# A two-block transformer kernel: the second block's first two projections from tokens that are not yet normed

## The chip, the cores and the metric

The kernel runs on one core of a Trainium2 chip. The metric is the device time of one execution in microseconds (us), as the median of several runs. TensorE (PE) multiplies matrices, VectorE (DVE) and ScalarE (ACT) work on elements, GpSimd (POOL) makes the low parts of the weights, and SyncE (SP) issues nearly all loads.

## The reference

256 tokens of 1024 go through a first block (gating, convolution, pooling, feed-forward, a gated embedding) and then through a second one (two kinds of attention, then 32 experts). The change lies at the border: the last step of the first block, and the norm and projection that begin the second.

```
def _rmsnorm(x, g):
    xf = x.astype(jnp.float32)
    y = xf * lax.rsqrt(jnp.mean(xf * xf, axis=-1, keepdims=True) + NORM_EPS)
    return (y * g.astype(jnp.float32)).astype(x.dtype)

def _modulate(h, shift, scale):
    return h * (1 + scale[:, None, :]) + shift[:, None, :]
...
        h = h + jax.nn.sigmoid(h @ w_ple_gate[i]) * (p[i] @ w_ple[i])
...
        h = _modulate(_rmsnorm(x, g_mix[layer]), shift_mix, scale_mix)
        qkv = h @ w_in[layer]
        q_d, k_d, v_d, q_s, k_s, v_s = jnp.split(
            qkv, [D_DIL, 2 * D_DIL, 3 * D_DIL, 3 * D_DIL + D_SB, 3 * D_DIL + 2 * D_SB], axis=-1)
```

`q_s` and `k_s` are the queries and keys of the stick-breaking attention, `q_d` and `k_d` those of the dilated one. For one token the norm is one number r (the inverse root), so a projection of the normed and modulated token is r times the projection of the token times the gain, plus the projection of the shift.

## The kernel before

Every engine has its own instruction list, written out by hand, and waits for the others by semaphores; nothing is scheduled by a planner. The order of the source is the order on each engine.

Products of weights and tokens are done three times, on high and low parts of both operands in the fast format fp32r: high x high, high x low, low x high (`product`, L552 to L554). So every activation matrix needs a high part (ScalarE's copy into the format) and a low part (VectorE's difference), and every weight block likewise (ScalarE's copy L1334, GpSimd's difference L2607). Weights stream through raw buffers and three split buffers; a split waits until the products of three blocks before are done, and ScalarE does two blocks ahead of TensorE (`take`).

The first block ends with `ple_gate`: four pieces of X (`part(n, tt, ...)`: weight part n, token half tt), four PSUM banks `gb`, numbered q = 2 * token half + column half. For each q ScalarE takes the sigmoid in PSUM (`gate`, L1630) and VectorE multiplies by the embedding and adds to X (`gated_embedding`, L2208 and L2210; the semaphore is `x_ok`); the order is q = 0, 2, 1, 3. X holds tokens on the partitions.

The second block begins as follows. TensorE turns the plain tokens (`turn_old`, L874, 16 transposes) for a later residual, which VectorE copies to SBUF as XTO (`old`, L2218). ScalarE sums squares by halves (`half_square`, L1613) and takes roots (`half_root`, L1620), VectorE inverts them. VectorE, and ScalarE for one quarter, multiply the tokens by the inverse root into XN (`normed`, L2235, L1647). TensorE turns XN (`turn_normed`, L887, 16 transposes); ScalarE and VectorE apply gain and shift (columns of MC) from PSUM into HF (L1662, L2248), ScalarE makes the high part (L1667), VectorE the low part (`low_of`, L1899). Then come the projections `qs0`, `ks0`, `qs1`, `ks1`, `qd0`, ... (`qk`, 48 products of 256 columns each, both output halves in one bank); ScalarE copies each result to QK (L1675). `sb_scores(0)` (L936, L937) needs qs0 and ks0; ScalarE's softplus on it is `sb_soft` (L1688 to L1692).

Where ScalarE's list is touched, the split of the ks0 weights has its second half behind the third norm:

```
            gate(1)
            assert begun[0] + 1 == next_split(first["ple_gate"] + 3)
            split_one(third_norm)
```

Behind the attention the experts' weights stream in; their loads wait for the places that the attention leaves.

Of the kernel before, what the change touches and what calls it, by code (L numbers as in the profile page):

```python
# [10 lines left out]
ALU = mybir.AluOpType  # L11
# [211 lines left out]
def program(nc, I, out, const_at):  # L223
    with ExitStack() as ctx:
# [85 lines left out]
        XN = ar(10240, 2048, 2)  # L310
        HF = ar(6144, 2048, 8)
# [81 lines left out]
        def tap(k, c):  # L393
# [24 lines left out]
        so4, so, soe = small(4), small(2), small(2)  # L418

# [14 lines left out]
                 ("norm3", 4), ("heads_s", 2), ("heads_d", 2))  # L434
# [7 lines left out]
         sbs_mm, sv_mm, di_mm, dt_mm, dv_mm, os_mm, xo_mm, cb_mm, ss_mm, rt_mm, hn_mm, rk_mm, ov_mm, xg_mm, gu_mm,  # L442
# [3 lines left out]
            "di_mm dt_mm dv_mm os_mm xo_mm cb_mm ss_mm rt_mm hn_mm rk_mm ov_mm xg_mm gu_mm turn_mm down_mm y0_mm y_mm "  # L446
            ).split())

        (warm_ok, nsq_ok, dg_ok, v_ok, sig_ok, vs_ok, u_ok, z_ok, g_ok, sq_ok, crs_ok, silu_ok, vnorm_ok, ple_ok, post_ok,
         cond_ok, ffa_ok, pg_ok, hfa_ok, qkv_ok, mr_ok, sbe_ok, die_ok, osq_ok, hs_ok,  # L450
         rs_ok, hn_ok, ex_ok, xga_ok, hsa_ok, fin_ok) = (
            sem(n) for n in (
            "warm_ok nsq_ok dg_ok v_ok sig_ok vs_ok u_ok z_ok g_ok sq_ok crs_ok silu_ok vnorm_ok ple_ok post_ok cond_ok "
            "ffa_ok pg_ok hfa_ok qkv_ok mr_ok sbe_ok die_ok osq_ok hs_ok rs_ok hn_ok ex_ok xga_ok "
# [3 lines left out]
        (blank_ok, rv_ok, vst_ok, vn_ok, glu_ok, tap_ok, cs_ok, wst_ok, tab_ok, mix_ok, pools_ok, cc_ok, cn_ok,  # L458
# [4 lines left out]
            "blank_ok rv_ok vst_ok vn_ok glu_ok tap_ok cs_ok wst_ok tab_ok mix_ok pools_ok cc_ok cn_ok bra_ok "  # L463
# [10 lines left out]
        qkv_at = {"qs0": 1, "ks0": 2, "qs1": 3, "ks1": 4, "qd0": 5, "kd0": 6, "qd1": 7, "kd1": 8, "vs": 10, "vd": 12}  # L474
# [42 lines left out]
        def tensor(e):  # L517
# [154 lines left out]
            def wst_sums():  # L672

                w.wait_ge(wst_ok, 1)
                for i in range(2):
# [4 lines left out]
                    free[b] = [(tab_ok, 4 * i + 4)]  # L680
# [178 lines left out]
            part(2, 1, True, True)  # L859
            part(3, 0, True, False)  # L860
            part(3, 1, True, True)
            bb = gb
            for q in range(4):
                free[bb[q]] = [(x_ok, x3(q))]
            held.update(bb)


            def turn_old(tt, half):

                w.wait_ge(x_ok, x3(2 * tt + half))  # L870
# [8 lines left out]
            def turn_normed(bb, tt):  # L879

                w.wait_ge(rv_ok, 8 + 2 * tt)
                for k in range(8):
                    if k == 4 and tt:
                        w.wait_ge(nsq_ok, 15)
# [165 lines left out]
            for kind in ("qs0", "ks0", "qs1"):  # L1050
                qk(kind)
# [1824 lines left out]
```

## Time and profile before

| | us |
|---|---|
| median of 3 runs | 1093.29 (1090.07 to 1094.33) |
| profiled execution, span from the first to the last instruction | 1089.9 |
| TensorE busy | 996.9 (91%) |
| VectorE busy | 528.6 (48%) |
| ScalarE busy | 391.9 (36%) |
| GpSimd busy | 498.4 (46%) |

The page gives the profiled execution by its span; no other time of that execution is listed. Shares of busy time are averages over stages with different limits, and TensorE's are modelled: what counts for a change is which wait ends last at its place. The border of the two blocks lies at 510 to 545 us of the span.

### The profile page before, as it was taken

The page shows a single profiled execution, that of the slowest core. Times are in us where ns is not written, and L with a number is a line of the kernel's source. Part 1 is how long each engine was busy: PE and PEld are TensorE (multiplying, and loading weights), DVE is VectorE, ACT ScalarE, POOL GpSimd, SP SyncE. Part 2 cuts the span into 40 slices and gives each one's busy share as a digit, 9 for nine tenths or more (in the row PEclk, how much of TensorE's full clock was granted, in tenths as well). Part 3 has the DMA queues.
Part 4 walks back from the last instruction along what each step waited for, and adds up shares of the span by engine and source line. Part 5 has one row for each costly group of instructions (what it writes and reads, how often), then busy time and mean ns, then how long its engine had stood idle before and what let it go on. Part 6 is the DMA issues. An engine that isn't in the chain of part 4 may idle for free.

```text
span 1089.9 us, 16602 instructions
## 1 busy us (share of the span) xinstructions
PE 996.9 (91%) x6894; PEld 736.4 (68%) x6894; DVE 528.6 (48%) x980; ACT 391.9 (36%) x559; POOL 498.4 (46%) x210
## 2 busy tenths in 40 slices
PE   7999999999999999999899999999959687859777
PEld 6989988788788888888798895544425243424333
DVE  1998896655367776214358554333213122212114
ACT  7345455554474544446597441000000000000003
POOL 5987699879498887888666510000000000000000
PEclk9999999999999999999999999999989898989889
DMA  9745455546469999638443889999999999999996
GB/s 380 281 166 185 148 201 192 173 190 267 173 232 396 362 362 373 263 116 325 144 155 116 351 347 416 429 425 428 425 429 425 434 427 424 431 426 426 431 422 255
DMA packets 36655, 341.96 MB, mean 314 GB/s; under 512 B 4065, under 2 KB 4449, under 8 KB 6114
## 3 DMA queue, kind: packets, MB, share of 16 engines
q1 hardware_dynamic: 35280, 337.82, 77.6%
q10 hardware_dynamic: 1298, 3.05, 0.7%
q8 instruction: 55, 0.90, 0.3%
q14 instruction: 22, 0.18, 0.0%
HBM read 339.81 MB, written 1.05 MB: 313 GB/s over the span
## 4 chain that ended last, share of the span: by engine, by line
PE 65%; DMA 25%; DVE 6%; ACT 3%; issue 1%; POOL 0%; DVEq 0%; SPq 0%; ACTq 0%
DMA body<-in_gu 21%; PE ps L552 15%; PE ps L554 15%; PE ps L553 15%; PE ps L1201 6%; PE ps L1243 4%; DMA body<-in_dn 4%; PE ps L1232 2%; PE ps L1182 1%; PE ps L734 1%; ACT sph L1334 1%; DVE ar L2314 1%; DVE ar L2308 1%; PE ps L1220 1%; PE ps L787 0%
## 5 line engine op out<-in xcount | busy, mean ns | idle before, releaser
L2607 POOL TENSOR_TENSOR spl<-raw,sph 128x1024 fp32r<-128x1024 f32 x204 | 496.4, 2466 | 139.5 <-ACT sph L1334 139.3
L1334 ACT ACTIVATE sph<-raw 128x1024 fp32r<-128x1024 f32 x204 | 208.3, 1055 | 109.1 <-PE ps L554 91.1
L2615 POOL TENSOR_SCALAR body<-body,SM 128x512 f32<-128x512 f32 x1 | 1.6, 1567 | 447.9 <-DVE SM L1874 447.9
L1826 ACT ACTIVATE ar<-ps 64x256 f32<-64x256 f32 x32 | 12.1, 377 | 332.9 <-PE ps L1201 332.9
L552 PE MATMUL ps<-sph,xbh 128*128 128x512 f32 x304 | 119.6, 394 | 0.4 <-DVE ar L2281 0.4
L554 PE MATMUL ps<-sph,xbl 128*128 128x512 f32 x304 | 118.5, 390 | 0.0
L553 PE MATMUL ps<-spl,xbh 128*128 128x512 f32 x304 | 118.4, 389 | 0.0
L1243 PE MATMUL ps<-ar,ar 128*128 128x512 f32 x240 | 111.6, 608 | 0.0
L552 PE MATMUL ps<-xah,sph 128*128 128x256 f32 x320 | 92.1, 288 | 0.4
L1919 DVE SCALAR_TENSOR_TENSOR ps<-ar,COL,ps 128x256 f32<-128x256 f32 x232 | 92.1, 482 | 0.0
L553 PE MATMUL ps<-xal,sph 128*128 128x256 f32 x320 | 90.5, 283 | 0.0
L554 PE MATMUL ps<-xah,spl 128*128 128x256 f32 x320 | 90.5, 283 | 0.0
L2558 DVE TENSOR_TENSOR ar<-ar,ps 64x256 f32<-64x256 f32 x32 | 13.6, 424 | 141.0 <-ACT ar L1826 141.0
L1243 PEld LDWEIGHTS ps<-ar,ar 128*128 128x128 f32 x240 | 45.4, 200 | 47.5 <-issue 47.5
L552 PE MATMUL ps<-sph,xah 128*128 128x512 f32 x192 | 75.7, 394 | 1.5 <-POOL spl L2607 1.5
L553 PE MATMUL ps<-spl,xah 128*128 128x512 f32 x192 | 74.8, 389 | 0.0
L554 PE MATMUL ps<-sph,xal 128*128 128x512 f32 x192 | 74.8, 389 | 0.0
L1201 PE MATMUL ps<-body,ar 128*32 128x256 f32 x656 | 46.7, 432 | 28.8 <-DMA body<-in_gu 28.8
L2495 DVE COPY ar<-ps 128x128 f32<-128x128 f32 x32 | 9.3, 292 | 127.1 <-PE ps L1220 127.0
L552 PEld LDWEIGHTS ps<-sph,xbh 128*128 128x128 f32 x304 | 57.1, 188 | 12.4 <-DVE ar L2281 0.8
L554 PEld LDWEIGHTS ps<-sph,xbl 128*128 128x128 f32 x304 | 57.1, 188 | 12.1
L553 PEld LDWEIGHTS ps<-spl,xbh 128*128 128x128 f32 x304 | 57.1, 188 | 11.5
(343 smaller groups left out, 1753.6 us busy)
## 6 DMA issues: line engine op xcount, KB each, us to landing
raw<-in_stream SPq DMA_DIRECT2D x127, 1024.0 KB, 5.7
body<-in_gu SPq DMA_DIRECT2D x11, 4096.0 KB, 47.3
body<-in_dn SPq DMA_DIRECT2D x15, 2048.0 KB, 45.7
body<-in_gu SPq DMA_DIRECT2D x10, 2048.0 KB, 25.5
body<-in_gu SPq DMA_DIRECT2D x14, 1024.0 KB, 10.6
body<-in_dn SPq DMA_DIRECT2D x12, 1024.0 KB, 11.9
tops<-in_gu SPq DMA_DIRECT2D x6, 2048.0 KB, 39.9
tops<-in_dn SPq DMA_DIRECT2D x4, 2048.0 KB, 47.8
```

The lines of the kernel that those rows point to most:

```text
L552: e.matmul(o, sh, mh, start=start, stop=False)
L553: e.matmul(o, sh, ml, start=False, stop=False)
L554: return e.matmul(o, sl, mh, start=False, stop=stop)
L734: mm = e.matmul(ps[b][:, d * 256:d * 256 + 256], WP[:, g, k, d * 128:d * 128 + 128], ZP[:, 2 * g + k, 16:272], start=(k == 0), stop=(k == 1))
L1201: mm = e.matmul(ps[b][32 * q:32 * q + 32, 0:256], XG[g % 2][:, k, (x % 4) * 32:(x % 4) * 32 + 32], W[:, q // 2, k % 2, (q % 2) * 256:(q % ...
L1232: mm = e.matmul(ps[b][32 * j:32 * j + 32, :], HE[x % 2][:, 32 * j:32 * j + 32], W[:, 2 * (j % 2) + j // 2, :], start=True, stop=True)
L1243: mm = e.matmul(ps[yb[tt * 2 + nn]][:, :], SWT[x % 2][:, tt * 128:tt * 128 + 128], YP[x % 2][:, nn * 512:nn * 512 + 512], start=False, sto ...
L1334: e.activation(u.half(SPH[u.n % NSP], h), u.half(RAW[u.slot], h), ACTF.Copy).then_inc(w.up(hi_ok), 1)
L1826: e.activation(HS[x % 2][0:64, :], ps[bank_of["gu", x]][0:64, 0:256], ACTF.Silu).then_inc(w.up(hsa_ok), 1)
L1919: e.scalar_tensor_tensor(out=acc if k < 30 else CVO[:, c, :], in0=CV[:, c, k:k + 256], scalar=tap(k, c), in1=acc, op0=ALU.mult, op1=ALU.add)\
L2558: e.tensor_tensor(h[0:64, :], h[0:64, :], ps[bank_of["gu", x]][64:128, 0:256], ALU.mult).then_inc(w.up(hsm_ok), 1)
L2607: e.tensor_tensor(u.half(SPLO[u.n % NSP], h), u.half(RAW[u.slot], h), u.half(SPH[u.n % NSP], h), ALU.subtract).then_inc(w.up(lo_ok), 1)
```

## The change

1. The tokens are turned once. `turn_plain` (16 transposes, the first eight ahead of the last two pieces of the gate product) puts the plain tokens into the four banks `norm3`, tokens on the free axis.
2. From there ScalarE and VectorE make high and low parts of token times gain, XU (`plain_high`, `plain_low`). Two more columns of XU hold the shift, so that a product has 258 columns.
3. qs0 and ks0 are projected from XU, each output half in its own bank, in pieces (`plain_part`). The inverse root is spread over the partitions by a product of ones with a diagonal (`diagonal3`, `spread_root3`) and copied to SBUF (RSB3). At the eviction VectorE multiplies by it and ScalarE adds the projected shift as a bias (`qk_plain`).
4. The normed tokens for the other projections are made in place in PSUM (`norm3`), the high part by ScalarE (`norm3_high`), the low part by VectorE (`norm3_low`). ScalarE copies the plain tokens out first (`keep_plain`).
5. XN, HF, `turn_normed`, `normed`, `turn_old` and `old` are gone. Some semaphores that were used once are merged.

TensorE's list ahead of and behind the first attention product. `xb` are the high and low tokens of the gate product, `sph` and `spl` split weights, `ar_106` is XN. Before:

```order
L553 MATMUL ps<-spl_63,xbh 128x512
L554 MATMUL ps<-sph_60,xbl 128x512
L874 MATMUL ps<-cst,X 128x128 [waits x_ok]
L874 MATMUL ps<-cst,X 128x128 x3
L874 MATMUL ps<-cst,X 128x128 [waits mc_ok,x_ok]
L874 MATMUL ps<-cst,X 128x128 x7
L874 MATMUL ps<-cst,X 128x128 [waits x_ok]
L874 MATMUL ps<-cst,X 128x128 x3
L887 MATMUL ps<-cst,ar_106 128x128 [waits rv_ok]
L887 MATMUL ps<-cst,ar_106 128x128 x7
```

The same place now, from the end of the gate product on (`xu_106` and `xu_107` are the high and low part of XU):

```order
L554 MATMUL ps<-spl_63,xbh 128x512
L555 MATMUL ps<-sph_60,xbl 128x512
L870 MATMUL ps<-cst,X 128x128 [waits x_ok]
L870 MATMUL ps<-cst,X 128x128 x3
L553 MATMUL ps<-xu_106,sph_61 128x258 [waits act_lo,lo_ok,x_ok]
L554 MATMUL ps<-xu_107,sph_61 128x258
L555 MATMUL ps<-xu_106,spl_64 128x258
```

The transposes of the normed tokens are gone, four transposes of plain tokens stand there, and the first product has a wait for x_ok of its own.

ScalarE's list from the second of the gate's sigmoids on (`sph_61` is the split of qs0's weights, `sph_59` that of ks0's). Before:

```order
L1630 ACTIVATE ps<-ps 128x512 [waits half_used]
L1334 ACTIVATE sph_61<-raw_53 128x8x128 [waits d_raw0]
L1334 ACTIVATE sph_61<-raw_53 128x8x128
L1613 ACTIVATE tmpa,SM<-X 128x512 [waits hi_ok,x_ok]
L1613 ACTIVATE tmpa,SM<-X 128x512 [waits nsq_ok,x_ok]
L1630 ACTIVATE ps<-ps 128x512 [waits tile0_mm]
L1334 ACTIVATE sph_59<-raw_54 128x8x128 [waits half_used,d_raw1]
L1613 ACTIVATE tmpa,SM<-X 128x512 [waits hi_ok,x_ok]
L1630 ACTIVATE ps<-ps 128x512 [waits half_used]
```

Now:

```order
L1640 ACTIVATE ps<-ps 128x512 [waits half_used]
L1344 ACTIVATE sph_61<-raw_53 128x8x128 [waits d_raw0]
L1344 ACTIVATE sph_61<-raw_53 128x8x128
L1655 ACTIVATE xu_106<-SM 128x8x2 [waits mc_ok]
L1651 ACTIVATE xu_106<-ps,SM 128x256 [waits xo_mm]
L1651 ACTIVATE xu_106<-ps,SM 128x256 x3
L1623 ACTIVATE tmpa,SM<-X 128x512 [waits act_hi,x_ok]
L1623 ACTIVATE tmpa,SM<-X 128x512 [waits nsq_ok,x_ok]
L1661 DMA cst<-in_wr 128x288
L1640 ACTIVATE ps<-ps 128x512 [waits tile0_mm]
```

Five copies, the first waiting for MC and the second for the turned tokens, and one DMA issue stand between the split and the third sigmoid.

VectorE's list from the first root's inverse (RECIPROCAL) to the second low part, before:

```order
L1874 RECIPROCAL SM<-SM 128x1 [waits x_ok,nsq_ok]
L2235 TENSOR_SCALAR ar_106<-X,SM 128x512 [waits rv_ok] x2
L1874 RECIPROCAL SM<-SM 128x1 [waits rv_ok,nsq_ok]
L2235 TENSOR_SCALAR ar_106<-X,SM 128x512 [waits rv_ok]
L2248 TENSOR_SCALAR ar_107<-ps,SM 128x256 [waits rv_ok,n_mm]
L2248 TENSOR_SCALAR ar_107<-ps,SM 128x256 [waits hf_ok]
L2248 TENSOR_SCALAR ar_107<-ps,SM 128x256 [waits hf_ok,n_mm]
L2248 TENSOR_SCALAR ar_107<-ps,SM 128x256 [waits hf_ok]
L1899 TENSOR_TENSOR xbl<-ar_107,xbh 128x512 [waits hf_ok,act_hi]
L1899 TENSOR_TENSOR xbl<-ar_107,xbh 128x512 [waits act_lo,act_hi] x3
```

Now, from the second root's inverse on (`ar_109` is RSB3):

```order
L1925 RECIPROCAL SM<-SM 128x1 [waits act_lo,nsq_ok]
L2293 COPY ar_109<-ps 128x256 [waits rv_ok,xo_mm]
L2301 SCALAR_TENSOR_TENSOR ps<-ps,SM,ar_109 128x256 [waits rv_ok,xo_ok]
L2301 SCALAR_TENSOR_TENSOR ps<-ps,SM,ar_109 128x256 [waits hf_ok]
L2301 SCALAR_TENSOR_TENSOR ps<-ps,SM,ar_109 128x256 [waits hf_ok,xo_ok]
L2301 SCALAR_TENSOR_TENSOR ps<-ps,SM,ar_109 128x256 [waits hf_ok]
L2308 SCALAR_TENSOR_TENSOR xbl<-ps,SM,xbh 128x256 [waits hf_ok,act_hi]
L2308 SCALAR_TENSOR_TENSOR xbl<-ps,SM,xbh 128x256 [waits act_lo]
L2301 SCALAR_TENSOR_TENSOR ps<-ps,SM,ar_109 128x256 [waits act_lo,xo_ok]
```

The whole row of steps on VectorE now stands behind the copy of the spread root, and it works from PSUM, 256 columns at a time.

The diff, cut to this place (the merged semaphores and the buffers are left out):

```diff
@@ tensor
             part(2, 1, True, True)
+            def turn_plain(tt, half):
+                w.wait_ge(x_ok, x3(2 * tt + half))
+                for k in range(4 * half, 4 * half + 4):
+                    b = bank_of["norm3", k // 2]
+                    o = (k % 2) * 256 + tt * 128
+                    if tt == 0 and k % 2 == 0:
+                        claim(b)
+                    mm = e.transpose(ps[b][:, o:o + 128], X[:, tt, k * 128:k * 128 + 128], ident)
+                mm.then_inc(w.up(xo_mm), 1)
...
+            nb3 = [bank(("norm3", n)) for n in range(4)]
+            held.update(nb3)
+            turn_plain(0, 0)
+            turn_plain(1, 0)
             part(3, 0, True, False)
             part(3, 1, True, True)
...
+            turn_plain(0, 1)
+            for kind in ("qs0", "ks0"):
+                for h in range(2):
+                    b = bank((kind, h))
+                    claim(b)
+                    held.add(b)
+            plain_part("qs0", range(4), True, False)
+            turn_plain(1, 1)
+            plain_part("ks0", range(4), True, False, (0,))
+            plain_part("qs0", range(4, 8), False, True)
+            spread_root3(bank_of["ks0", 1])
+            plain_part("ks0", range(4, 8), False, True, (0,))
+            w.wait_ge(rv_ok, 8)
+            plain_part("ks0", range(8), True, True, (1,))
@@ scalar
             take(first["ple_gate"] + 2)
+            w.wait_ge(mc_ok, 3)
+            e.activation(XU[0][:, :, 256:258], MC[:, 0:8].unsqueeze(2).broadcast_to((128, 8, 2)), ACTF.Copy)\
+                .then_inc(w.up(act_hi), 1)
+            plain_high(0)
             half_square(0, 0)
             half_square(1, 0)
...
             gate(1)
             assert begun[0] + 1 == next_split(first["ple_gate"] + 3)
-            split_one(third_norm)
+            split_one(last_gate)
+            warm(ACTF.Sqrt)
+            half_root(0)
+            plain_high(1)
+            half_square(1, 1)
+            half_root(1)
+            diagonal3(0)
...
+            keep_plain(0)
+            diagonal3(1)
+            keep_plain(1)
+            split_one(first_tokens)
+            for k in range(4, 8):
+                norm3_high(k)
+            take(first["ks0"])
+            qk_plain("qs0")
+            qk_plain("ks0")
+            qk("qs1")
@@ vector
             gated_embedding(0)
             gated_embedding(2)
...
+            plain_low(0)
...
             gated_embedding(3)
             w.wait_ge(nsq_ok, 12)
             invert(ss3[:, 0:1], rv_ok)
+            plain_low(1)
             w.wait_ge(nsq_ok, 14)
             invert(ss3[:, 1:2], rv_ok)
+            w.wait_ge(xo_mm, 5)
+            e.tensor_copy(RSB3, ps[bank_of["ks0", 1]][:, 0:256]).then_inc(w.up(rv_ok), 1)
...
+            norm3(0)
+            norm3(1)
+            norm3_low(0)
+            norm3(2)
+            norm3_low(1)
+            norm3(3)
+            norm3_low(2)
+            norm3_low(3)
+            qk_plain("qs0")
+            qk_plain("ks0")
```

## Rows read from the trace of the kernel before

**Rows 1.** Timeline of TensorE: start us, us, engine line, operands, count, idle before
```profile
510.72 0.39 PE L552 MATMUL ps<-sph,xbh 128*128 128x512 f32 x1
...
516.17 1.48 PE L874 MATMUL ps<-cst,X 128*128 128x128 f32 x12
518.46 0.65 PE L874 MATMUL ps<-cst,X 128*128 128x128 f32 x4 [0.82 <-DVE X L2210]
520.14 1.97 PE L887 MATMUL ps<-cst,ar 128*128 128x128 f32 x16 [1.03 <-DVE ar L2235]
525.18 0.54 PE L552 MATMUL ps<-xbh,sph 128*128 128x256 f32 x1 [3.07 <-DVE xbl L1899]
...
528.29 0.41 PE L554 MATMUL ps<-xbh,spl 128*128 128x256 f32 x1
528.50 0.34 PE L552 MATMUL ps<-xbh,sph 128*128 128x256 f32 x1
...
529.99 0.28 PE L552 MATMUL ps<-xbh,sph 128*128 128x256 f32 x1
530.11 0.28 PE L553 MATMUL ps<-xbl,sph 128*128 128x256 f32 x1
```
**Rows 2.** Chain of waits that ended last, in order of time: start us, us, what
```profile
513.64 0.59 ACT ps L1630
...
520.14 1.32 PE ps L887 x10
...
544.18 0.64 PE ps L936 x4
...
608.32 1.73 PE ps L1013 x8
```
**Rows 3.** Stretches, TensorE alone: us, busy (count), granted clock, DMA share, GB/s
```profile
522.00:525.00 3.00, 0.11 (x1) 1.00 0.02 6
526.00:527.00 1.00, 1.00 (x6) 0.50 0.72 262
```
**Rows 4.** Timeline of ScalarE
```profile
508.69 2.00 ACT L1334 ACTIVATE sph<-raw 128x1024 fp32r<-128x1024 f32 x2
510.78 0.63 ACT L1613 ACTIVATE tmpa<-X 128x512 f32<-128x512 f32 x1
511.32 0.19 ACT L1613 ACTIVATION_READ_ACCUMULATOR tmpa<-X 128x1 f32 x1
...
547.65 1.49 ACT L1688 ACTIVATE ar<-ar 128x1536 f32<-128x1536 f32 x1 [0.94 <-DVE ar L2260]
...
557.53 0.60 ACT L1675 ACTIVATE ar<-ps 128x512 f32<-128x512 f32 x1 [0.33 <-PE ps L554]
```
**Rows 5.** Groups of ScalarE, 0 to 200 us: count | busy us, mean ns | idle before
```profile
L1362 ACT ACTIVATE xah<-ps,COL 128x256 fp32r<-128x256 f32 x8 | 3.1, 472 | 0.7 <-PE ps L546 0.7
```
**Rows 6.** Timeline of VectorE
```profile
517.71 0.69 DVE L2210 TENSOR_TENSOR X<-X,ps 128x512 f32<-128x512 f32 x1
...
612.36 2.08 DVE L2325 SCALAR_TENSOR_TENSOR ps<-ps,COL,cst 128x256 f32<-128x256 f32 x4
```
**Rows 7.** Timeline of TensorE, the only split products of other widths
```profile
571.12 0.39 PE L948 MATMUL ps<-lbl,ou 128*128 128x384 f32 x1
571.34 0.22 PE L949 MATMUL ps<-lbl,ou 128*128 128x128 f32 x1
```
**Rows 8.** Two lines of VectorE: ns shortest/median/longest, first and last start, forms
```profile
L1889 DVE SCALAR_TENSOR_TENSOR xal<-ps,COL,xah x16: 483/484/486, 12.8 to 232.3; 128x256 fp32r<-128x256 f32 x16
...
L1899 DVE TENSOR_TENSOR xbl<-ar,xbh x8: 692/1314/2716, 234.2 to 526.7; 128x512 fp32r<-128x512 f32 x8
```
**Rows 9.** The page's costliest groups, GpSimd
```profile
L2607 POOL TENSOR_TENSOR spl<-raw,sph 128x1024 fp32r<-128x1024 f32 x204 | 496.4, 2466 | 139.5 <-ACT sph L1334 139.3
```
**Rows 10.** Timeline of TensorE among the experts
```profile
817.30 1.93 PE L1201 MATMUL ps<-body,ar 128*32 128x256 f32 x32 [2.33 <-DMA body<-in_gu]
...
875.98 2.92 PE L1201 MATMUL ps<-body,xg 128*32 128x256 f32 x32 [2.62 <-DMA body<-in_gu]
```

More of the change, by code:

```diff
@@ new lines, in plain_part @@
+            def plain_part(kind, ks, start, stop, halves=(0, 1)):
+                u = units[first[kind]]
+                H, L = k8(SPH[u.n % NSP]), k8(SPLO[u.n % NSP])
+                for h in halves:
+                    b = bank_of[kind, h]
+                    c = slice(h * 128, h * 128 + 128)
+                    w.wait_ge(lo_ok, 2 * u.n + h + 1)
+                    for k in ks:
+                        w.wait_ge(act_lo, part_at["plain3"] + k + 2)
+                        mm = product(ps[b][:, 0:258], H[:, k, c], L[:, k, c], XU[0][:, k, :], XU[1][:, k, :],
+                                     start and k == ks[0], stop and k == ks[-1])
+                    if stop:
+                        mm.then_inc(w.up(half_used), 1)
+                        free[b] = [(qkv_ok, qkv_at[kind])]
@@ L868, in turn_old @@
-            def turn_old(tt, half):
-                w.wait_ge(x_ok, x3(2 * tt + half))
-                b = bank(("xo", tt, half))
-                claim(b)
-                for k in range(4 * half, 4 * half + 4):
-                    mm = e.transpose(ps[b][:, (k % 4) * 128:(k % 4) * 128 + 128], X[:, tt, k * 128:k * 128 + 128],
-                                     ident)
-                mm.then_inc(w.up(xo_mm), 1)
-                free[b] = [(xo_ok, 2 * tt + half + 1)]
[L879 to L884, printed above, removed]
-                    o = (k % 2) * 256 + tt * 128
-                    claim(bb[k // 2])
-                    mm = e.transpose(ps[bb[k // 2]][:, o:o + 128], XN[:, tt, k * 128:k * 128 + 128], ident)
-                    if k == 7 or (tt and k % 2):
-                        mm.then_inc(w.up(n_mm), 1)
@@ L909, in tensor @@
-            x_att = landed("norm3", 1)
+                free[gb[q]] = [(x_ok, x3(q))]
+            held.difference_update(gb)
+            turn_plain(0, 1)
[8 more added lines that the diff above has]
+            plain_part("qs0", range(4, 8), False, True)
@@ L911, in qk @@
+            spread_root3(bank_of["ks0", 1])
+            plain_part("ks0", range(4, 8), False, True, (0,))
+            w.wait_ge(rv_ok, 8)
+            plain_part("ks0", range(8), True, True, (1,))
+            for n in range(4):
+                free[nb3[n]] = [(act_lo, part_at["norm3"] + 2 * n + 2)]
+            held.clear()
+            x_att = landed("norm3", 2)
             def qk(kind):
```

199 lines of the change are left out of this document (99 added, 100 removed).

## The prediction, made before any run of the changed kernel

> **What bounds the kernel now.** I read the chain of waits first, then TensorE's own timeline, then the other engines' around the same place. The reader is to see that the changed place is on the chain and how little of it is there. Up to 516.17 TensorE streams the last gate product without a gap; then 32 transposes follow in three pieces, and the first attention product starts at 525.18, after waits of 0.82, 1.03 and 3.07 us [rows 1]. The chain goes through exactly these pieces: the sigmoid, then the transposes of the normed tokens [rows 2], then the subtraction that makes their low parts (L1899), which ends the last wait [rows 1]. So 525.18 - 516.17 = 9.0 us stand between two dense stretches, and the first 3.3 us of the second one run at a granted clock of 0.50, that is 1.2 GHz [rows 3]: a step of 0.21 us between products where it is 0.12 later [rows 1]. Some 15 products lie in it, so it costs about 15 x 0.09 = 1.4 us. All in all 10.4 us could be hidden at most, 0.95% of the span. From 525 TensorE is dense to the scores at 544.18 [rows 2], and at 557.53 ScalarE still waits for it (0.33 us) [rows 4]; the whole attention part hangs on when these products end.
>
> **The change part by part, on the clock of the profiled execution.**
>
> *The start.* TensorE turns the first eight plain tiles before the last two pieces of the gate product instead of behind them. At 1.97 / 16 = 0.123 us each [rows 1] this puts 8 x 0.123 = 1.0 us in front: the product that starts at 510.72 starts at 511.7, and its end goes from 516.17 to 517.15.
>
> ScalarE gets new work ahead of the second gate: a small copy (about 0.2) and four scaled copies of 256 columns. Such copies take 0.472 each, and 8 of them fill 3.1 us, so 0.39 a step [rows 5]. It is free at 510.69 (behind the splits of 508.69) but waits for the turned tiles until about 511.9; the copies end at 513.4, the two squares of 0.82 (0.63 and 0.19 for reading the sum; the first stood at 510.78 before) end at 515.0 [rows 4]. So the sigmoid that stood at 513.64 [rows 2] starts at 515.0: 1.3 us later. What is queued behind it is the rest of the chain of the last tokens: add, split, sigmoid, add. VectorE's last add of the embedding, which ended at 518.40 [rows 6], ends at 519.7.
>
> *The wait in the middle.* The order shows that the first product on plain tokens waits for x_ok as well as for its operands, behind four transposes that have waited for the third quarter. PSUM has eight banks: four hold the turned tokens, so the four banks of the two projections are those of the gate product, and all four are claimed before the first product. The last of them is free only when the last quarter of the tokens is added, 519.7. So TensorE does four transposes (517.15 to 517.65) and then stands for 2.1 us. So of the 9.0 us between the dense stretches 519.8 - 517.15 = 2.65 remain, and no work of TensorE covers more of it, since every later instruction is queued behind this claim.
>
> *The two projections.* 96 products with 258 columns. No row has that size; between the 0.12 step of 256 columns [rows 1] and the 0.22 step of 384 [rows 7] I take 0.12, from which it is two columns away. Then, counting on: 24 products (2.9) to 522.7, four transposes to 523.2, 12 products to 524.6. The second half of the plain tokens is made only now: ScalarE's four copies start at 523.4 and end at 525.0, VectorE's four low parts follow at 0.52 each (2.08 / 4 [rows 6], the same form) and end at 526.3. TensorE, ready at 524.6, trickles behind them and is through the first projection at 528.2. The roots, in the shadow of this, are ready at 527.2. The spreading product is one fp32 product of 256 columns; four such made 8 instructions in 1.73 us [rows 2], so 0.43: 528.6, landed at 528.8, copied to SBUF by 529.3. The second projection ends at 532.9. Before, two projections ended at 538.2 by the same steps: **TensorE is 5.3 us ahead here**.
>
> *The normed tokens.* This is the new bound. From 529.3 VectorE has 16 dependent steps on 256 columns in PSUM (8 in place, 8 low parts), with ScalarE's eight high parts (0.39 each), its copies of the plain tokens and the split of the third weight fitting in between: 16 x 0.52 = 8.3, so the last pair lands at 537.6. The third projection wants it in pairs: ready at 532.9, it trickles to 538.4, then does its second half (24 x 0.12 = 2.9) to 541.2. So 2.5 of the 5.3 us are given back, a wait of VectorE in the place of the old one. The before kernel's costly steps here (L1899, both inputs in SBUF, 0.69 to 2.7 us [rows 8]) and its copies of old tokens on VectorE are gone, which the sum contains.
>
> *The evictions with roots.* VectorE's four one-column copies and four products with the spread roots come behind the 16 steps: about 4 x 0.7 = 2.8 (0.52 for the product, 0.2 an estimate for the copy; 4.2 if both cost 0.52), to 540.4, and ScalarE's last of four copies ends at 540.9. The scores start at 541.3, against 544.18 [rows 2]: **2.8 us**. ScalarE then has two splits of 2.0 and a copy of 0.5 queued ahead of the softplus (take for the third and fourth projection), which starts at 545.3 and not at 547.65 [rows 4]: **2.4 us**. GpSimd's share of these splits (2.47 each half [rows 9]) ends at 547 for the weight that TensorE wants at 548.7, so it is hidden by 1.7 us; were it late, its excess would go on the path. At 557.53 the two paths meet, one 2.4 and the other 2.8 us earlier; I take 2.6.
>
> *What becomes of it.* From there on the order is the same, and each engine's work is released by the others', ScalarE to 575, VectorE behind it. The loads of expert weights that follow start as the attention part frees their places, and the long last stretch waits for those loads (2.33 and 2.62 us idle, ended by DMA in_gu [rows 10]). All of it starts 2.6 us earlier, so the end does. Merging semaphores costs nothing: the waits stay where they were.
>
> *A rule on the clock.* Between 516.17 and 522.1 TensorE did transposes only, and the clock was still granted in full until it had stood for 3.07 us [rows 1, 3]. The Trainium skill's page "TensorE: Matmul & The Clock Gate", section "Part 4: PE-mode transpose", says that transposes do not count as work for the clock as products do. By that rule it would be at half when the projections start at 519.8, and the gain 1.4 us smaller, 1.2; the trace of before does not agree with it, and the sum goes by the rows.
>
> **The rivals.**
> *The clock falls inside the new block.* TensorE stands for 2.1 us behind half a microsecond of transposes. After 2.33 us idle 32 products took 1.93 (full), after 2.62 they took 2.92 [rows 10]. The new gap lies just under the first. If it falls, the first products cost 1.4 us more, and with them the second half of the tokens and all behind it: gain 1.2, **1092.1**. The same price if it falls while the third projection trickles.
>
> *The 258 columns are dear.* At the 0.22 of 384 columns the 60 products ahead of the spreading product cost 60 x 0.10 = 6 us more, of which 1 falls into the wait for the second half of the tokens; the scores would start near 547.8, 3.6 us later than before: **1097**, slower. It decides against the change from a step of about 0.165. For it: none of the split products in the trace (L552 to L554, L948, L949) has a size that is no multiple of 128. Against it: 256 columns go at their full rate.
>
> *The chain of 16 steps is dearer.* If they wait for GpSimd's reads, as L1899 did, from 0.70 a step the gain is gone; at 0.79 it is **1095**. Against it: L1889, with one input in PSUM as here, took 483 to 486 ns wherever it stood [rows 8].
>
> *It does better.* Were TensorE's gap and the trickle smaller by half (the sigmoids earlier because the squares fit into the wait for the tiles, the steps at 0.49), the gain would be 4: **1089**.
>
> *It doesn't do what it says.* That the projections hardly overlap the norm, with no gain at all, **1093**, would need the wait for the last bank and both trickles to be longer by 2.6 us in all.
>
> **How the numbers follow.** The profiled span is 1089.9; the shown runs have 1090.07 to 1094.33, median 1093.29. Nothing in the sum depends on what lies around the span, so the 2.6 us come off the median: 1093.29 - 2.6 = 1090.7. Chances: the forecast (gain 1.8 to 3.4) 0.57, the clock 0.17, better 0.09, no gain 0.05, dearer steps 0.06, dear columns 0.06. The shown runs differ by 4 us, so a new median can lie 2 us from the old one with nothing changed. The range 1087.5 to 1095.0 takes in all but the dear columns and part of the dear steps and of the spread. A measurement of this kernel tells about 0.5% (5.5 us) from no change. More than that faster needs more than half of the 10.4 us: 0.07. More than that slower needs the dear columns at a worse step than 0.22, or steps of 0.9 and more: 0.04. The same: 0.89.
>
> **What would show it.** Right: TensorE's first product on the plain tokens near 519.8, ended by VectorE's last add to X; the third projection's first half in pairs behind VectorE; its first matmul near 533; scores near 541.3; softplus near 545.2; and everything behind 557 earlier by 2.6 us. Wrong: a step other than 0.12 with 258 columns; a granted clock of 0.5 between 520 and 542; the 16 steps of VectorE not near 0.52; or a first product well before the last add, which would mean that I misread the claim of the banks.

## The result, and the profile after

The changed kernel takes 1096.60 us (median of 10 runs, 1095.15 to 1098.56) against 1092.53 before (median of 10 runs beside them, 1089.93 to 1094.33): a ratio of 1.0042, 95% interval 1.0034 to 1.0051. It is slower by 4.1 us. The forecast was 2.6 us faster, and the time lies above the range's upper end of 1095.0. The size of the change, 0.42%, is under the 0.5% that the chances were set by, so "the same" (0.89) came out, but not for the reason that the forecast gave: the sign is the other one.

The profiled execution after spans 1095.8 us, 5.9 more than the one of before. I followed the chain of waits forward. TensorE's timeline first (start us, us, engine and line, operands, count, and in brackets the idle time before it and what ended it):

```profile
519.76 0.39 PE L553 MATMUL ps<-xu,sph 128*128 128x258 f32 x1 [2.04 <-DVE X L2261]
519.99 0.28 PE L554 MATMUL ps<-xu,sph 128*128 128x258 f32 x1
520.11 0.28 PE L555 MATMUL ps<-xu,spl 128*128 128x258 f32 x1
...
521.41 0.42 PE L553 MATMUL ps<-xu,sph 128*128 128x258 f32 x1
521.62 0.42 PE L554 MATMUL ps<-xu,sph 128*128 128x258 f32 x1
...
529.86 0.59 PE L892 MATMUL ps<-ar,cst 128*128 128x256 f32 x2
...
539.91 0.58 PE L553 MATMUL ps<-xbh,sph 128*128 128x256 f32 x1 [5.12 <-DVE xbl L2308]
540.29 0.41 PE L554 MATMUL ps<-xbl,sph 128*128 128x256 f32 x1
540.50 0.41 PE L555 MATMUL ps<-xbh,spl 128*128 128x256 f32 x1
...
548.10 0.71 PE L947 MATMUL ps<-ar,ar 64*128 64x256 f32 x4
...
610.47 1.83 PE L1008 MATMUL ps<-cst,ar 128*128 128x128 f32 x15 [0.15 <-DVE ar L2391]
```

and two rows of the same engine before, the scores and the place that answers to 610.47:

```profile
544.11 0.71 PE L936 MATMUL ps<-ar,ar 64*128 64x256 f32 x4
...
606.49 1.83 PE L997 MATMUL ps<-cst,ar 128*128 128x128 f32 x15 [0.20 <-DVE ar L2314]
```

The rows answer to [rows 1] and to the scores of [rows 2]. Where before has three waits and then a dense stretch, after has two: 2.04 us for the last quarter of the tokens, and **5.12 us ahead of qs1**, the third projection, which the forecast had trickling in pairs (a pair is two of the eight slices k of 128 features; it lies in one bank). Behind each wait the step between products is 0.21 us instead of 0.12 (521.41 to 521.62, 540.29 to 540.50). The stretches of the same engine say why (from:to, us, busy and count, granted clock, DMA share, GB/s):

```profile
521.00:523.00 2.00, 2.00 (x12) 0.54 0.38 66
...
540.00:545.00 5.00, 5.00 (x24) 0.50 0.41 174
```

The clock fell to 1.2 GHz twice, where before has one such fall [rows 3]. VectorE, whose sixteen steps (L2301 in place, L2308 low parts) make the normed tokens:

```profile
519.02 0.69 DVE L2261 TENSOR_TENSOR X<-X,ps 128x512 f32<-128x512 f32 x1
...
530.50 0.42 DVE L2293 COPY ar<-ps 128x256 f32<-128x256 f32 x1 [2.32 <-PE ps L892]
531.02 2.15 DVE L2301 SCALAR_TENSOR_TENSOR ps<-ps,SM,ar 128x256 f32<-128x256 f32 x4
...
537.74 2.11 DVE L2308 SCALAR_TENSOR_TENSOR xbl<-ps,SM,xbh 128x256 fp32r<-128x256 f32 x4
```

And ScalarE behind the scores:

```profile
551.65 1.49 ACT L1721 ACTIVATE ar<-ar 128x1536 f32<-128x1536 f32 x1 [0.94 <-DVE ar L2337]
...
561.52 0.60 ACT L1708 ACTIVATE ar<-ps 128x512 f32<-128x512 f32 x1 [0.31 <-PE ps L555]
```

The scores start at 548.10 against 544.11 before (544.18 in the chain of waits, [rows 2]): 4.0 us later. The softplus (551.65 against 547.65) and the copy at 561.52 (557.53) [rows 4] are 4.0 later too, and at 610.47, where before has 606.49, it is still 4.0. That is the 4.1 us of the medians. The 1.9 that the two profiled spans differ by beyond it lie behind 610, among the experts, where one execution stands against one (the ten spans of after go from 1093.0 to 1096.4).

So all of it lies between the last add and the scores. In the sections below a kernel is read by two distances that don't depend on where its execution stood before: from the start of the last add to X (L2261 and its like) to VectorE's copy of the spread roots, and from the same start to the scores. After they are 530.50 - 519.02 = 11.48 and 548.10 - 519.02 = 29.08 us; before, the scores stand 544.11 - 517.71 = 26.40 behind the last add, which is itself 1.3 us earlier. Times in the profiles of different kernels can also be shifted as a whole by half a microsecond, which these distances leave out. Two of the kernels below were profiled twice, and their distances came out the same to 0.02 us (24.64 and 24.63, 21.93 and 21.92 to the scores), so tenths can be read.

### The profile page after: what moved, and what is told of

Same layout as the page of the kernel before. It is cut to its first block, busy times and chain, and to the rows that moved or that the text cites. A ratio compares the mean times of both kernels' runs of the same rounds, so it can differ in the third digit from the quotient of the medians.

```text
span 1095.8 us, 16617 instructions
## 1 busy us (share of the span) xinstructions
PE 1000.2 (91%) x6880; PEld 738.0 (67%) x6880; DVE 535.1 (49%) x999; ACT 396.7 (36%) x575; POOL 498.4 (45%) x210
## 4 chain that ended last, share of the span: by engine, by line
PE 69%; DMA 18%; DVE 7%; ACT 3%; issue 1%; another core or an unknown queue 1%; POOL 0%; DVEq 0%; ACTq 0%; SPq 0%
DMA body<-in_gu 17%; PE ps L553 15%; PE ps L555 15%; PE ps L554 15%; PE ps L1211 8%; PE ps L1253 6%; PE ps L1242 3%; PE ps L1192 1%; PE ps L1230 1%; PE ps L735 1%; DVE ar L2391 1%; ACT sph L1344 1%; PE ps L1226 1%; PE ps L788 0%
```

## The experiments

**The theory.** To claim a PSUM bank is to wait until its last reader is done. Two claims make TensorE wait where its operands are there, and each of these waits is followed by a fall of the clock. The first claim I knew: all four banks of the two plain projections are claimed before the first product, so the first product waits for the last add. The second I had missed. qs1's bank comes from the rotation, which gives out the banks in turn and stands at bank 7 at that place; that bank holds the last pair of the turned tokens, and is free only when the last low part of it has been made. The order of the program shows it: of the rows of qs1's first half only the first waits for the tokens (a row has line, operands and semaphores waited for; these are the first seven).

```
L553 MATMUL ps<-xbh,sph_60 128x256 [waits lo_ok,act_lo]
L554 MATMUL ps<-xbl,sph_60 128x256
L555 MATMUL ps<-xbh,spl_63 128x256
L553 MATMUL ps<-xbh,sph_60 128x256
L554 MATMUL ps<-xbl,sph_60 128x256
L555 MATMUL ps<-xbh,spl_63 128x256
L553 MATMUL ps<-xbh,sph_60 128x256
```

Had the products waited for their operands, the seventh row, the first of the second pair, would wait for act_lo again; it doesn't, since a later value has been waited for. The rivals: VectorE's longer chain is the cost whatever the bank (then another bank only turns one long wait into a slow trickle), and the falls of the clock have another cause than the waits.

**The bank of qs1.** One line added, which sets the rotation back to the bank of the first pair (and with it shifts the banks of all that follows):

```diff
             held.clear()
             x_att = landed("norm3", 2)
+            turn_at[0] = nb3[0]
```

> The changed kernel with one line more: the third projection (qs1) takes the bank of the first pair of normed tokens (norm3 0) instead of that of the last pair (norm3 3). Theory A (the claim of the bank is what makes TensorE stand until all 16 steps of VectorE are done): the first product of qs1 moves from 539.91 to about 534.5, right behind the first two low parts; three quarters of the first half are done when the last pair lands at 539.9, so the scores start at 543.5 if the granted clock stays full and near 545.7 if it falls to 0.5 once more, against 548.1; median 1092 to 1094. Rival B (the tokens themselves are late, the bank is not asked for before them): the first product stays at 539.9 and the scores at 548, median 1096.6.

Measured: 1091.42 us against 1091.66 before, ratio 0.9997, interval 0.9988 to 1.0007. The one line takes back the whole loss. TensorE's timeline of this kernel, then VectorE's last add:

```profile
519.20 0.58 PE L553 MATMUL ps<-xu,sph 128*128 128x258 f32 x1 [2.04 <-DVE X L2262]
...
535.97 0.39 PE L553 MATMUL ps<-xbh,sph 128*128 128x256 f32 x1 [1.06 <-DVE xbl L2309]
...
538.21 0.39 PE L553 MATMUL ps<-xbh,sph 128*128 128x256 f32 x1 [1.26 <-DVE xbl L2309]
...
543.10 0.71 PE L948 MATMUL ps<-ar,ar 64*128 64x256 f32 x4
```
```profile
518.46 0.69 DVE L2262 TENSOR_TENSOR X<-X,ps 128x512 f32<-128x512 f32 x1
```

The 5.12 us became two waits of 1.06 and 1.26, between pairs, as the forecast had them. The scores stand 543.10 - 518.46 = 24.64 us behind the last add instead of 29.08: 4.4 us sooner. What is expected of 18 more products made in the shadow of VectorE (18 x 0.12 = 2.2) and of 24 products no longer at half the clock (24 x 0.09 = 2.2) is 4.4. The rival that the chain of VectorE costs the same with any bank is out. The 2.04 us are still there.

**The claim ahead of the first product.** ks0's two banks are claimed only after qs0's first half of k and the four transposes behind it:

```diff
                 for h in range(2):
                     b = bank((kind, h))
-                    claim(b)
+                    if kind == "qs0":
+                        claim(b)
                     held.add(b)
             plain_part("qs0", range(4), True, False)
             turn_plain(1, 1)
+            for h in range(2):
+                claim(bank_of["ks0", h])
```

> The changed kernel with the banks of the second projection (ks0) claimed behind its last four transposes, where TensorE has waited for the last quarter of the tokens anyway, and not ahead of the first product. Theory A: the first product on plain tokens moves from 519.76 to 517.7, TensorE no longer stands for 2 us there, the granted clock stays at 1.0 until 525, the copy of the spread root is done near 527.5 and not 530.9; but TensorE then stands longer ahead of the third projection (which still waits for all the normed tokens, near 536.4), starts it at half clock, and the scores come at 544.5: median 1093. Rival B (the second half of the plain tokens, not the claim, sets the pace): the copy of the root stays within 1 us of 530.9, scores at 547 to 548, median 1096.

Measured: 1092.27 us, ratio to before 1.0003, interval 0.9994 to 1.0012. TensorE's timeline, then VectorE's last add and copy of the roots:

```profile
517.16 0.36 PE L553 MATMUL ps<-xu,sph 128*128 128x258 f32 x1
...
535.76 0.58 PE L553 MATMUL ps<-xbh,sph 128*128 128x256 f32 x1 [5.12 <-DVE xbl L2311]
...
543.57 0.71 PE L950 MATMUL ps<-ar,ar 64*128 64x256 f32 x4
```
```profile
518.70 0.69 DVE L2264 TENSOR_TENSOR X<-X,ps 128x512 f32<-128x512 f32 x1
...
526.35 0.42 DVE L2296 COPY ar<-ps 128x256 f32<-128x256 f32 x1 [2.33 <-PE ps L892]
```

The 2.04 us are gone, and so is the first fall of the clock. The copy of the roots stands 526.35 - 518.70 = 7.65 us behind the last add instead of 11.48, which is 3.8: about 2.3 of it the wait itself (the first product stands 0.74 us behind the start of the last add before the edit, 1.54 ahead of it now), and 1.5 the fall. The scores gain 4.2 (24.87 instead of 29.08), since of the fall behind the unchanged 5.12 us a little less is left (20 products instead of 24). The time came out near what was expected. The copy of the roots came 1.1 and the scores 0.9 us sooner, and the wait ahead of qs1, which was expected to grow, stayed at 5.12.

**Both.** The two edits together.

> Both of the above. Theory A: first product at 517.7, copy of the root at 527.5, VectorE's 16 steps end at 536.4, the third projection trickles from 531 on, scores at 539.9 (before: 544.1) if the clock holds, 542 if it falls once; median 1088.5 to 1090.5, faster than before. Rival B: as the changed kernel, 1096.

Measured: 1088.89 us, ratio to before 0.9970, interval 0.9958 to 0.9982: faster than either edit alone. TensorE's timeline and one stretch of it, then VectorE's last add and ScalarE:

```profile
532.69 0.39 PE L553 MATMUL ps<-xbh,sph 128*128 128x256 f32 x1 [1.06 <-DVE xbl L2312]
...
534.92 0.49 PE L553 MATMUL ps<-xbh,sph 128*128 128x256 f32 x1 [1.26 <-DVE xbl L2312]
540.92 0.71 PE L951 MATMUL ps<-ar,ar 64*128 64x256 f32 x4
```
```profile
535.00:540.00 5.00, 5.00 (x30) 0.66 0.61 210
```
```profile
518.99 0.69 DVE L2265 TENSOR_TENSOR X<-X,ps 128x512 f32<-128x512 f32 x1
```
```profile
544.47 1.49 ACT L1725 ACTIVATE ar<-ar 128x1536 f32<-128x1536 f32 x1 [0.79 <-DVE ar L2341]
```

The scores stand 21.93 behind the last add; they start 3.2 us ahead of before, and the softplus 3.2 (547.65, [rows 4]), and the medians differ by 2.8. So the forecast's 2.6 us were there to be had; the two claims and the falls behind them had taken them. A fall of the clock is left, behind the idle 1.26 us this time: the granted clock of 535 to 540 is 0.66. With one fall the scores had been expected at 542; they came 1.1 us sooner.

**Is the fall brought by the idle time? Products in the first wait.** 26 unused products of 128 columns stand in the changed kernel's 2.04 us:

```diff
             turn_plain(0, 1)
+            w.wait_ge(lo_ok, 2 * units[first["qs0"]].n + 1)
+            w.wait_ge(act_lo, part_at["plain3"] + 2)
+            for _ in range(26):
+                e.matmul(ps[nb3[2]][:, 128:256], k8(SPH[units[first["qs0"]].n % NSP])[:, 0, 0:128],
+                         XU[0][:, 0, 0:128], start=True, stop=True)
             for kind in ("qs0", "ks0"):
```

> The changed kernel with 26 products of 128 columns whose results are not used (they go to places that the last transposes overwrite) in the wait of 2.04 us ahead of the first product on plain tokens. Theory A (the fall of the granted clock at 521.2 comes from this wait, and costs 1.3 us): granted clock 1.0 from 519 to 525, the copy of the spread root done near 529.6 and not 530.9, scores 1.3 us earlier than 548.1. Rival C (the fall comes from somewhere else, or costs nothing since TensorE waits for the tokens' second half anyway): clock 0.5 as before at 521 to 524.6, or the copy of the root stays at 530.9.

Measured once: 1097.32 us (changed kernel 1095.15 to 1098.56). TensorE's timeline and a stretch of it, then VectorE's copy of the roots:

```profile
517.39 3.10 PE L907 MATMUL ps<-xu,sph 128*128 128x128 f32 x26
520.33 0.33 PE L553 MATMUL ps<-xu,sph 128*128 128x258 f32 x1
```
```profile
521.00:523.00 2.00, 2.00 (x19) 1.00 0.40 66
```
```profile
529.47 0.42 DVE L2297 COPY ar<-ps 128x256 f32<-128x256 f32 x1 [2.32 <-PE ps L892]
```

The clock stayed at 1.00. The 26 products took longer than the wait they fill: the first real product starts 520.33 - 518.93 = 1.40 behind the last add instead of 0.74. So of the 1.5 us of the fall 0.9 reach the roots' copy (10.54 behind the last add instead of 11.48) and 0.65 the scores (28.43). That is half of what was expected, and too little for one time to show: the place in the profile decides here, not the time.

**The same with transposes.** 16 further transposes in the place of the products:

```diff
             turn_plain(0, 1)
+            for _ in range(4):
+                for k in range(4, 8):
+                    o = (k % 2) * 256
+                    e.transpose(ps[nb3[k // 2]][:, o:o + 128], X[:, 0, k * 128:k * 128 + 128], ident)
             for kind in ("qs0", "ks0"):
```

> Edit against the changed kernel: 16 further transposes of the first token tile (the same transposes as the four ahead of them, written again to the same place, so nothing else changes) stand in TensorE's queue in the 2.04 us in which it waits for the last quarter. Sixteen at some 0.13 us each (four took 0.66 in the timeline, the first one's start-up in it) are about 2.0 us. It is the twin of the run with 26 unused products there, in which the granted clock of 519 to 525 stayed at 1.00 and the roots' copy on VectorE came 0.94 us sooner after the last add (10.54 against 11.48). Theory A, that the clock falls because TensorE stands idle, with whatever kind of instruction the idle time is filled: clock 1.00 from 519 to 525, no product 0.21 apart, roots' copy 10.5 to 10.9 us behind the last add, scores about 547.3. Rival B, that transposes don't count as work for the clock (the Trainium skill, 'TensorE: Matmul & The Clock Gate', 'Part 4: PE-mode transpose', says so of them): the clock falls as in the changed kernel or sooner, 0.5 to 0.6 somewhere in 518 to 525, roots' copy 11.4 us or more behind the last add, scores 548 or later. The median says little at one look: 1095 to 1098 by either.

Measured once: 1095.71 us. TensorE's timeline and a stretch of it, then VectorE's last add and copy of the roots:

```profile
516.93 1.91 PE L907 MATMUL ps<-cst,X 128*128 128x128 f32 x16
519.13 0.39 PE L553 MATMUL ps<-xu,sph 128*128 128x258 f32 x1 [0.29 <-DVE X L2265]
```
```profile
521.00:523.00 2.00, 2.00 (x19) 1.00 0.45 102
```
```profile
518.39 0.69 DVE L2265 TENSOR_TENSOR X<-X,ps 128x512 f32<-128x512 f32 x1
...
528.33 0.42 DVE L2297 COPY ar<-ps 128x256 f32<-128x256 f32 x1 [2.32 <-PE ps L892]
```

Idle 0.29 us, and the clock stays at 1.00. The roots' copy stands 528.33 - 518.39 = 9.94 behind the last add, the scores 27.50: 1.54 and 1.58 us sooner, more than was expected. So the first fall costs 1.5 us, all of it on the path, and filling the wait with transposes alone takes it away. The Trainium skill says in "TensorE: Matmul & The Clock Gate", "Part 4: PE-mode transpose", that transposes don't count as the engine's work in the same way; for these 16 between two runs of products the measurement decides, and it says that they held the clock.

**The kernel with both claims mended, once more, beside a version of it.**

> The kernel with both banks' claims mended, once more, beside the next run on the same chip. In its first profile the qs1 products trickled with idles of 1.06 and 1.26 us and the clock then fell from 534.9 to 538.4 (16 products 0.21 apart, about 1.5 us), while the kernel with the bank alone mended had the same two idles at 1.00 throughout. Theory A, that the fall belongs to this kernel (what TensorE did before it is the same in each execution): the fall is there again at the same place, scores 21.9 us behind the last add, median 1088.3 to 1089.5, faster than before by 0.2 to 0.45%. Rival B, that it comes or not by chance from one execution to the next: clock 1.00 from 535 to 540 this time, scores about 20.4 behind the last add.

Measured: 1088.84 us, ratio to before 0.9971, interval 0.9960 to 0.9981, the same as the first time. The fall is there again: the stretch of 535 to 540 has a granted clock of 0.66 in both profiles, and the scores stand 540.84 - 518.92 = 21.92 behind the last add. So neither the fall nor the gain was an accident of one execution.

The version gives qs1's two halves two banks and takes the second half's products pair by pair with the first's, so that 12 instead of 30 are left when the last low part lands:

```diff
+            def qk_in_step(kind):
+                u = units[first[kind]]
+                H, L = k8(SPH[u.n % NSP]), k8(SPLO[u.n % NSP])
...
+                for pair in range(4):
+                    for h in range(2):
+                        if pair < h:
+                            continue
+                        c = slice(h * 128, h * 128 + 128)
+                        w.wait_ge(lo_ok, 2 * u.n + h + 1)
+                        if pair == h:
+                            claim(nb3[h])
+                        for k in range(0 if pair == h else 2 * pair, 2 * pair + 2):
+                            w.wait_ge(*x_att(k))
+                            mm = product(ps[nb3[h]][:, 0:256], H[:, k, c], L[:, k, c], XB[0][:, k, :],
+                                         XB[1][:, k, :], k == 0, k == 7)
...
-            qk("qs1")
+            qk_in_step("qs1")
             sb_scores(0)
+            held.discard(nb3[1])
```

> Edit against the kernel with both claims mended: the two halves of qs1 go into two banks, and the second half's products follow the first half's pair by pair instead of after all of them, so that 12 products instead of 30 are left when the last low part lands. ScalarE evicts qs1 in two instructions of some 0.47 us instead of one of 0.59. By the first profile of that kernel the last low pair lands at 535.97; 12 products are 1.4 us at full clock or 2.6 at the lower one, so qs1 ends at 537.4 to 538.6, before the last root eviction on ScalarE (539.39), which then ends last: scores at 539.5 instead of 540.92. The second idle of 1.26 us is filled by 12 products of the second half, so the clock should not fall at 534.9. Theory A: of these 1.4 us only about 0.6 reaches the softplus, because ScalarE's own queue stands before it: root eviction to 539.4, two weight conversions to 541.2, the qs1 evictions to 541.9, two conversions to 543.9, softplus at 543.9 instead of 544.47; median 0.6 below the kernel with both claims mended, about 1088.3. Rival B, the lead reaches the softplus whole: softplus at 543.0 to 543.1, median 1.4 below it, about 1087.5. Rival C, it gives nothing or less, because the held bank delays the scores or their successors: scores at 540.9 or later, median 1089 or more.

Measured: 1087.89 us, ratio to before 0.9961, interval 0.9947 to 0.9974. This is the lowest median of all, 0.95 us below that of the kernel with both claims mended beside it, but the two intervals overlap, so the times don't tell the two apart. TensorE, then ScalarE:

```profile
534.09 0.39 PE L553 MATMUL ps<-xbh,sph 128*128 128x256 f32 x1 [0.52 <-POOL spl L2719]
...
534.66 0.41 PE L553 MATMUL ps<-xbh,sph 128*128 128x256 f32 x1
534.87 0.41 PE L554 MATMUL ps<-xbl,sph 128*128 128x256 f32 x1
...
540.10 0.71 PE L976 MATMUL ps<-ar,ar 64*128 64x256 f32 x4
```
```profile
541.62 2.02 ACT L1374 ACTIVATE sph<-raw 128x1024 fp32r<-128x1024 f32 x2
543.64 1.49 ACT L1756 ACTIVATE ar<-ar 128x1536 f32<-128x1536 f32 x1
```

Half of the expectation held. The second half could not fill the wait behind the second pair: GpSimd's split of its weight (L2719) ended only then, so TensorE stood another 0.52 us, and the clock fell all the same: from 534.66 the step is 0.21. The scores gained 0.7 us on the kernel with both claims mended that ran beside it (540.10 against 540.84), not 1.4. But the softplus starts at 543.64 against 544.38 there, with no idle time before it: ScalarE's two conversions stand in front of it, as expected, so a further gain of TensorE's would not have reached it.

**The last fall.** In the kernel with both claims mended, 9 unused transposes stand ahead of qs1 and 10 ahead of its fifth slice k:

```diff
                     for k in range(8):
+                        if name == "qs1" and h == 0 and k in (0, 4):
+                            for _ in range(9 if k == 0 else 10):
+                                e.transpose(ps[b][:, 256:384] if k == 0 else ps[nb3[1]][:, 0:128],
+                                            X[:, 0, 0:128], ident)
                         if ready:
                             w.wait_ge(*ready(k))
...
```

> Edit against the kernel with both claims mended: 9 unused transposes of a token tile (128 columns, some 0.12 us each) stand ahead of qs1's first product and 10 ahead of its fifth k, so that the two idles of 1.06 and 1.26 us between pairs are filled (9 x 0.12 = 1.1 and 10 x 0.12 = 1.2). In the two profiles of that kernel the granted clock fell from 534.9 to 538.4, behind the second of these idles, and 16 products ran 0.21 apart instead of 0.12 (about 1.5 us). Theory A, idle TensorE brings the fall here as it did in the gate's wait: no idle of more than 0.3 us between 527 and 541, clock 1.00 from 535 to 540, the 30 products behind the last pair end at 539.5 instead of 540.8, scores at 539.6 to 539.8, the softplus at 543.5 to 543.9 (ScalarE's conversions stand before it), median 0.4 to 0.9 below 1088.9. Rival B, the fall there has another cause than these idles (the kernel with the bank alone mended had the same idles and no fall): the clock falls again between 534 and 539, scores at 540.9 or later, median 1088.5 to 1090.

Measured: 1088.24 us, ratio to before 0.9973, interval 0.9964 to 0.9983. TensorE's timeline and stretch, then ScalarE:

```profile
530.67 1.15 PE L575 MATMUL ps<-cst,X 128*128 128x128 f32 x9
...
533.42 1.26 PE L575 MATMUL ps<-cst,X 128*128 128x128 f32 x10
539.74 0.71 PE L956 MATMUL ps<-ar,ar 64*128 64x256 f32 x4
```
```profile
535.00:540.00 5.00, 4.87 (x38) 1.00 0.62 210
```
```profile
543.49 1.48 ACT L1730 ACTIVATE ar<-ar 128x1536 f32<-128x1536 f32 x1
```

No fall, the scores 1.1 us sooner (540.84 in the unfilled kernel), the softplus 0.9 sooner and now without idle time before it. The profile agrees with the theory (the idle time brings the fall) at each point. The median is 0.6 below that of the unfilled kernel, but that one stood against other runs of before; the ratios, 0.9973 and 0.9971 with intervals of about 0.001 to either side, are not told apart. So the gain is shown at the softplus and not in the time.

**The bank alone, a second profile.**

> The kernel with the bank alone mended, a second profile: in the first its clock fell behind the gate's wait (519 to 522) and stayed at 1.00 behind the idles of 1.06 and 1.26 us in qs1, at which the kernel with both claims mended fell twice in two profiles. Theory A, that what went before decides (each kernel does the same in each execution): again 0.55 to 0.60 somewhere in 519 to 523 and 1.00 from 535 to 545, scores 24.6 us behind the last add. Rival B, chance from one execution to the next: the clock falls behind these idles this time, scores 26 us behind the last add.

Measured once: 1091.31 us. Stretches of TensorE:

```profile
519.00:521.00 2.00, 1.26 (x8) 0.88 0.19 80
521.00:523.00 2.00, 2.00 (x12) 0.50 0.36 57
...
535.00:540.00 5.00, 2.55 (x17) 1.00 0.20 39
```

As the first time: a fall behind the 2.04 us, none behind the 1.06 and 1.26 us, scores 543.63 - 519.00 = 24.63 behind the last add. Not all was the same: the first time the product right behind the wait was slow already (0.58 us at 519.20), this time the step was 0.12 at first, and 0.22 from 520.60 on. Whether the short idles bring a fall looks like a property of the kernel: the kernel with the bank alone had none in either of its two profiles, the kernel with both claims had one in each of its two. Two profiles of each speak against chance and don't exclude it. What in the work ahead would decide it was not tried and stays open.

## Why the prediction was wrong

Point by point, the forecast's clock against the trace of after:

| step | forecast | after |
|---|---|---|
| ScalarE's four copies start | 511.9 | 511.71 |
| last add to X ends | 519.7 | 519.71 |
| wait ahead of the first plain product | 2.1 | 2.04 |
| first plain product | 519.8 | 519.76 |
| step of 258 columns at full clock | 0.12 | 0.12 |
| roots copied by | 529.3 | 530.92 |
| 16 steps of VectorE | 8.3 | 8.93 |
| first product of qs1 | 532.9 | 539.91 |
| scores | 541.3 | 548.10 |
| softplus | 545.2 to 545.3 | 551.65 |

**Right.** The start, to two tenths of a microsecond: the shift of the gate, the squares, the last add, the claim of the four banks with its wait, and the price of 258 columns. The rival of dear columns, which was the one that ended slower by the most, is out: 520.11 - 519.99 = 0.12. That its 1097 lies next to the 1096.60 measured is chance. Its price was thin as well: products of 512 columns step 0.23 before (510.49 to 510.72), about the 0.22 that the forecast read for 384. Right too was that what is gained or lost at the scores stays whole to the end of the attention part.

**Wrong, in order of size.** The 6.8 us between 541.3 and 548.10 come apart so.

- *"ready at 532.9, it trickles to 538.4"*: 2.2 us, and the cause of as much again. This is the step that failed. I asked of qs1 what its operands need, and not which bank it writes. I had read the claims of the first two projections, where the code names them; that of the third is hidden in the rotation. The trace of before could not show it; the order did, by the wait that the seventh row lacks. 18 products that should have run beside VectorE ran behind it. The kernel with qs1's bank set back shows the trickle just as forecast.
- *The clock at qs1*: 2.2 us, 24 products at 0.21 instead of 0.12. It hangs on the same claim, and went with it (24.64 against 29.08). The forecast had it among the rivals ("the same price if it falls while the third projection trickles"), at 1.4 us.
- *The clock at the first products*: 1.5 us. The forecast weighed this as a rival at 0.17 and took the side of the row in which 32 products behind 2.33 us idle ran at full clock [rows 10]. That one row was too thin: the 2.04 us were followed by a fall in all three profiles that have them unfilled. With 16 transposes in the wait the copy of the roots came 1.54 us sooner.
- *VectorE's steps*: 0.6 us. They were sized at 0.52 from start to start; within a run of four they are 0.54 (2.15 / 4), and where a run of one kind gives way to the other about 0.1 more passes (533.27 - 531.02 = 2.25 for four, against 2.15 busy).

The remaining 0.3 are the first product at the lower clock and the rounding. The two claims decide the sign: with either one mended the change is level with before (0.9997 and 1.0003), and with both it is 2.8 and 3.3 us faster in two measurements. That this is close to the 2.6 of the forecast is in part luck, since it comes together otherwise (the first wait, which the forecast had left in, gone; a fall, which it had not, in).

**The range.** Its upper end held one fall of the clock; two falls and a claim came, and they were not independent, since each of the two waits brought its own fall. The rival "it doesn't do what it says" named longer waits "by 2.6 us in all" as its condition and gave it 0.05: its mechanism was nearer than its price.

## What to carry to other kernels

Where banks or buffers are given out by a rotation, read for each consumer which one it gets, and when its last reader is done: a wait for a buffer can undo an overlap that the operands allow. An order printed with its waits shows it: a row that should wait again and doesn't has waited for something later already. And price a wait of TensorE with the clock behind it, here 2.0 us of waiting with 1.5 us of slow products, and 5.1 with 2.2; work that needs nothing, even repeated transposes, took the second part away in the first of these waits; in the longer one it was not tried.

## What the runs showed of the hardware that I had not expected

- 16 fp32 transposes of 128 columns (0.12 us each) in a wait of TensorE's held the granted clock at 1.00 as products did, and 19 in two other waits did too; without them it fell to 0.54 and 0.66.
- Two idles of 1.06 and 1.26 us, with six products between them, were followed by a fall of the clock in one kernel, in two profiles of two, and by none in another, in two of two; idles of 1.07 and 0.52 us in a third were followed by one. Idle time alone as I read it from the rows does not say whether the clock will fall.
- The fall need not follow at once: behind the same 2.04 us the first product was slow already in one profile of the kernel with the bank alone mended (519.20), the seventh was the first slow one in the other (520.60, 0.86 us behind the wait), and the twelfth in the changed kernel (521.19, 1.43 us behind it).
